# Feed-forward blocks: three pairs of weight tiles in each computed as seven block products

## What is computed

```
D_FF = 2816
def swiglu(h, w_in, w_out):
    gate, up = jnp.split(h @ w_in, 2, axis=-1)     # h 256 x 1024, w_in 1024 x 5632
    return (jax.nn.silu(gate) * up) @ w_out         # w_out 2816 x 1024

for l in range(2):
    x = x + 0.5 * swiglu(rms_norm(x, ffn_norm[l, 0]), ffn_w_in[l, 0], ffn_w_out[l, 0])
    ...   # layer 0: RWKV time mix; layer 1: differential attention
    x = x + 0.5 * swiglu(rms_norm(x, ffn_norm[l, 1]), ffn_w_in[l, 1], ffn_w_out[l, 1])
    ...   # after layer 0: keys and values shared with layer 1 (kv)
```

## Time and profile before

| | us |
|---|---|
| runs shown: median (lowest, highest) | 2159.72 (2157.41, 2160.54) |
| profiled execution, its own time | 2161.44 |
| span of the profile, first to last instruction | 2159.4 |
| PE busy | 1912.5 |
| DVE busy | 1319.4 |
| ACT busy | 809.6 |

### The profile page before, as it was taken

How to read it: one execution, slowest core, us unless ns; L and a number is a source line. 1 busy time by engine, 2 the same in 40 slices (tenths; PEclk the granted TensorE clock), 3 DMA queues, 4 the chain that set the end, 5 groups by cost and what they waited for, 6 DMA issues and landing times.

```text
span 2159.4 us, 30419 instructions
## 1 busy us (share of the span) xinstructions
PE 1912.5 (89%) x11687; PEld 1397.2 (65%) x11687; DVE 1319.4 (61%) x2197; ACT 809.6 (37%) x1285; POOL 604.0 (28%) x650
## 2 busy tenths in 40 slices
PE   7999777887776677678999999999999999989999
PEld 4997753443222222224888888988887788778887
DVE  4877695665656666645554757455456654586444
ACT  3336231322212112112444555335435444475443
POOL 1000266666667666665000001323000000021000
PEclk9999999999999999999999999999999999989999
DMA  9983499999999999997755321035555555415553
GB/s 353 359 271 98 161 349 382 364 354 371 356 367 376 348 378 369 357 379 294 241 192 189 120 90 52 5 114 181 186 183 175 177 193 187 163 59 176 190 182 115
DMA packets 251470, 510.35 MB, mean 236 GB/s; under 512 B 14810, under 2 KB 165036, under 8 KB 248284
## 3 DMA queue, kind: packets, MB, share of 16 engines
q0 software_dynamic: 74416, 270.83, 33.2%
q1 hardware_dynamic: 173802, 233.95, 32.9%
q10 hardware_dynamic: 3138, 4.00, 0.6%
HBM read 507.68 MB, written 1.05 MB: 236 GB/s over the span
## 4 chain that ended last, share of the span: by engine, by line
PE 60%; POOL 12%; DVE 8%; issue 8%; DMA 7%; ACT 3%; another core or an unknown queue 2%; ACTq 0%; SPq 0%; DVEq 0%; POOLq 0%
PE bank_pair L760 21%; PE bank_pair L794 11%; PE bank_pair L443 9%; POOL big L1978 7%; PE bank_pair L1850 5%; DMA big<-in_peer_v,aux 2%; POOL hf L1978 2%; POOL aux L1978 2%; PE bank_pair L3225 2%; PE bank_pair L2720 1%; DMA big<-in_peer_u,aux 1%; DMA big<-in_w_mod 1%; DVE big L2096 1%; DVE w_lo L354 1%
## 5 line engine op out<-in xcount | busy, mean ns | idle before, releaser
L354 DVE TENSOR_TENSOR w_lo<-w_raw,w_hi 128x2048 fp32r<-128x2048 f32 x196 | 449.1, 2292 | 257.8 <-ACT w_hi L349 257.4
L349 ACT ACTIVATE w_hi<-w_raw 128x2048 fp32r<-128x2048 f32 x196 | 374.5, 1912 | 216.4 <-PE bank_pair L760 107.4
L1850 PE MATMUL bank_pair<-big 128*128 128x512 f32 x676 | 337.8, 627 | 110.1 <-DMA big<-in_peer_v,aux 72.9
L1850 PEld LDWEIGHTS bank_pair<-big 128*128 128x128 f32 x676 | 119.6, 194 | 307.6 <-DMA big<-in_peer_v,aux 167.7
L760 PE MATMUL bank_pair<-w_hi,hh 128*128 128x512 f32 x704 | 277.5, 396 | 3.1 <-DVE x L1654 1.7
L2096 DVE SCALAR_TENSOR_TENSOR big<-big,bank_pair 128x1024 f32<-128x1024 f32 x172 | 208.8, 1217 | 114.9 <-DMA big<-in_peer_u,aux 97.8
L760 PE MATMUL bank_pair<-w_lo,hh 128*128 128x512 f32 x704 | 273.1, 390 | 0.0
L760 PE MATMUL bank_pair<-w_hi,hl 128*128 128x512 f32 x704 | 265.6, 390 | 0.2 <-DVE hl L695 0.2
L1978 POOL DMA_INDIRECT big<-in_peer_v,aux x172 | 165.7, 963 | 104.7 <-issue 45.9
L1978 POOL DMA_INDIRECT big<-in_peer_u,aux x172 | 164.0, 954 | 72.7 <-issue 47.9
L1963 ACT ACTIVATE big<-ident,aux 128x128 f32<-128x128 f32 x252 | 84.3, 390 | 259.1 <-issue 91.9
(11 more groups left out here) (516 smaller groups left out, 3285.6 us busy)
## 6 DMA issues: line engine op xcount, KB each, us to landing
w_raw<-in_ffn_w_in SPq DMA_DIRECT2D x176, 512.0 KB, 4.6
w_raw<-in_ffn_w_out SPq DMA_DIRECT2D x44, 1024.0 KB, 4.9
big<-in_w_mod SPq DMA_DIRECT2D x24, 1024.0 KB, 8.1
w_raw<-in_w_in SPq DMA_DIRECT2D x22, 1024.0 KB, 9.6
w_raw<-in_rwkv_w_rkv SPq DMA_DIRECT2D x12, 1024.0 KB, 5.6
w_raw<-in_peer_w_query SPq DMA_DIRECT2D x8, 1024.0 KB, 5.9
w_raw<-in_w_kv SPq DMA_DIRECT2D x8, 1024.0 KB, 5.2
w_raw<-in_w_out SPq DMA_DIRECT2D x4, 1024.0 KB, 5.3
```

The lines of the kernel that those rows point to most:

```text
L349: act.activation(to, w_raw[i][:, :], ACT.Copy).then_inc(S("w_hi"), 1)
L354: dve.tensor_tensor(lo, w_raw[i][:, :], hi.bitcast(F32), ALU.subtract).then_inc(S("w_lo"), 1)
L1850: mm = pe.matmul(bank[4 + 2 * tt + half][:, :], diag[:, r % VDIAGS, :], ring_rows[turn % RROWS][:, half * 512:(half + 1) * 512], start=(r ...
```

## The change

In each block, tiles 2 and 3, 5 and 6, 8 and 9 become pairs ("wide" tiles); tiles 0, 1, 4, 7 and 10 stay as they were. For a pair, the 256 x 1024 tokens are seen as 2 x 2 blocks (token half, half of the width) and the 1024 x 1024 weights as 2 x 2 blocks (half of the width; 512 gate or 512 up columns). The result's four blocks come from seven block products in place of eight, each of 12 matmuls:

- the slots of a pair are `b11`, `t1`, `t2`, then `down` of the tile before, then `t3`, `b21`, `t4`, `b22`; the next slots are gate and up of the ordinary tile and the two `down` of the pair. `ffn_slots` lists them, and the loops over tiles are written out.
- `t1` and `t3` are sums of two blocks of weights: SP loads one, and POOL issues a DMA that adds the other on arrival (`wide_pool`, `accum_op=ALU.add`). `t2 = t1 + b22` and `t4 = t2 + b21` are added by DVE (`wide_sum`). These blocks have buffers of their own beside the ring; they are split into the ring's slots. SP loads seven blocks where there were four slots, two of them by way of POOL.
- The sums of token blocks are made once in a block: eight copies on ACT ahead of the root, four operations on DVE (`token_sums`), one split on each engine.
- DVE puts the results together from the banks with five operations of 128 x 512 per pair (`partial`), and `gate_copy` on ACT keeps one product.
- `distance_pool` comes after the first two adding DMAs of block 1, `lora_loads` after those of block 0. The second half of the keys is turned right after the first, in banks 6 and 7, and copied out by DVE in block 2. In block 3 the first two `turn_residual` come after the gate and up products of the last tile.
- The last `down` slot is split ahead of the last copies and the last rest.

```diff
+FFN_UNITS = {f: [("R", i) for i in range(FTILES)] if f not in WIDE_FFNS else
+             [("R", 0), ("R", 1), ("S", 2), ("R", 4), ("S", 5), ("R", 7), ("S", 8), ("R", 10)] for f in range(4)}
...
+        def wide_pool(pool, f, tiles):
+            for tile in tiles:
+                for step in ("t1", "t3"):
+                    wide_landed(pool, step, f, tile)
+                    pool.dma_start(wide_raw[f][step].rearrange("p (k c) -> p k c", k=4),
+                                   wide_block(f, tile, *WIDE_ADDED[step]), accum_op=ALU.add)                        .then_inc(S(f"{step}_added"), 16)
...
+            def wide_products(tile):
...
+                block(tile, "b11", 0, *of_tokens(0, 0), True, False)
+                pe.wait_ge(S("token_sum"), EARLIER["token_sum"] + WIDE_FFNS.index(f) + 1)
+                block(tile, "t1", 3, *of_sums(0), True, False)
+                block(tile, "t2", 1, *of_sums(1), True, False)
+                n = SLOT[f, "o", tile - 1]
+                down_wait(n, tile - 1)
+                for part in range(4):
+                    mm = down(n, n % WRING, False, False, part)
+                mm.then_inc(S("slot_done"), 1)
+                summed(1)
+                block(tile, "t3", 1, *of_sums(2), False, False)
+                pe.wait_ge(S("gate_copy"), EARLIER["gate_copy"] + w + 1)
+                block(tile, "b21", 0, *of_tokens(0, 1), False, True)
+                summed(2)
+                block(tile, "t4", 1, *of_tokens(1, 1), False, True)
+                summed(3)
+                block(tile, "b22", 3, *of_sums(3), False, True)
...
+            def ordinary_products(tile):
...
+                gate_up(n, 0, n % WRING, (0, 2))
+                wide_turn(tile - 2)
+                gate_up(n + 1, 1, (n + 1) % WRING, (0, 2))
+                wide_down(tile - 2)
+                wide_down(tile - 1)
+                turn_act(tile, 2)
...
+            def token_sums():
...
+                o(dve.tensor_tensor(first, a21, a22, ALU.subtract))
+                o(dve.tensor_tensor(third, a11, a21, ALU.subtract))
+                o.wait()
+                o(dve.tensor_tensor(second, first, a11, ALU.subtract))
+                o.wait()
+                o(dve.tensor_tensor(fourth, a12, second, ALU.add))
...
+                for tile in (2, 5, 8):
...
+                    lo.upto(at + 4)
+                    partial(tile, 1)
+                    wide_sum("t4", tile)
+                    lo.upto(at + 6)
+                    partial(tile, 2)
+                    partial(tile, 3)
+                    lo.upto(at + 8)
+                    partial(tile, 4)
+                    lo.upto(at + 9)
+                    partial(tile, 5)
+                    wide_mult(tile)
```

More of the change, by code:

```diff
@@ L40 @@
 FTILES = FF // CW
+WIDE_FFNS = (0, 1, 2, 3)
 LORA, LORA_G = 64, 160
@@ L268, in slot_loads @@
         def slot_loads(n):
-            return 2 if any(n - BASE[f"ffn{f}"] in range(32) and (n - BASE[f"ffn{f}"]) % 3 != 1 or n == BASE[f"ffn{f}"] + 1
-                            for f in range(4)) else 1
+            if n not in FFN_SLOT:
+                return 1
+            return {"g0": 2, "g1": 2, "o": 1}.get(FFN_SLOT[n][1], 0)
         def slot_landed(n):
@@ L785, in gate_up, with down @@
                 mm.then_inc(S("slot_done"), 1)
-            def down(n, r, first, last, part):
+            def down(n, r, first, last, part, wide_tile=None):
                 a_hi, a_lo = (last_hi, last_lo) if last else (act_hi[:, :], act_lo[:, :])
+                if wide_tile is not None:
+                    a_hi, a_lo = (wide_act[f][part_of][wide_tile % 3 == 0] for part_of in range(2))
                 wh, wl = (w[r][:, :].rearrange("p (a d) -> p a d", a=2) for w in (w_hi, w_lo))
@@ L895, in ffn_act @@
             hi.upto(base + 2)
+            if f in WIDE_FFNS:
+                for k in range(KT):
+                    a = act.activation(fm(token_flat)[:, k, :], xf[:, k, :], ACT.Copy, scale=col(GAIN[norm], k))
+                a.then_inc(S("token_sum_hi"), 1)
             if norm in SUMS:
@@ L3257, in kv_pe @@
             keys_turn_pe(pe, 0)
+            for b in range(2):
+                pe.wait_ge(S(f"proj_free{b}"), (projection_number(KV) + 1 - b) // 2 + 4)
+            keys_turn_pe(pe, 1)
         def kv_act(act, hi):
```

375 lines of the change are left out of this document (319 added, 56 removed).

## The result

The changed kernel takes 2143.62 us (median of six runs, 2138.17 to 2149.45); the kernel before took 2159.12 beside it (2155.63 to 2162.18). The ratio is 0.9926, 95% interval 0.9908 to 0.9943: 15.5 us less by the medians, where 27 had been forecast. The profiled execution is the fastest of the six, 2138.17 us with a span of 2136.4, so 1.8 of it lie outside the span.

The account below looks back on a forecast made before the run. The prediction took PE to bound the kernel, busy all 130 of 130 us in mid-block. Its terms, -34.0 + 1.2 + 3.6 + 1.0 + 0.9 = -27.3 us, led from 2161.4 to 2134.1, forecast as 2132 us, range 2127 to 2148.

## What to carry to other kernels

Draw the balance of DMA time for the start of a stage, not only for its steady cycle: count what must land by the second round, with each adding transfer at its own price (here twice a plain one), from the moment at which the first load may really go out. Here the low-rank loads, moved behind others while the engines were full, were paid for by the transfer that came next; they cost nothing where the share was low. And small work on DVE cost nothing in the gap where it waited for ACT, and its full length on the path, though DVE was busy only 81% of the time.
